# A streaming encoder step on one core: rope by copies, normalised tiles in step, and a first gate product in three passes

## What is computed

```
for i in range(2):
    x += 0.5 * swiglu(rmsnorm(x), w_ffn1)        # gate and up 1024 x 2816, down 2816 x 1024
    x += mixer_i(rmsnorm(x))                     # i = 0: latent attention, i = 1: retention
    x += 0.5 * swiglu(rmsnorm(x), w_ffn2)
y = rmsnorm(x)

def rope(x, pos):                                # x1, x2 are the halves of the last axis
    return concatenate([x1 * cos - x2 * sin, x1 * sin + x2 * cos])
```

## Time and profile before

| | |
|---|---|
| median of 3 runs | 1680.11 us (1679.96 to 1680.40) |
| the profiled execution, whole | 1680.21 us |
| its span, first to last instruction | 1678.4 us |
| PE busy | 1643.5 us, 98% of the span, 9523 matmuls |
| weight loads of PE | 1583.1 us, beside the matmuls |
| DVE busy | 822.8 us, 49% |
| ACT busy | 636.1 us, 38% |
| POOL busy | 287.4 us, 17% |
| mean granted clock of PE | 0.996 |
| share of PE in the chain that ended last | 94% |

### The profile page before, as it was taken

One profiled execution on the slowest core, in us unless ns is written; L12 is line 12 of the kernel. 1 busy time (PEld: TensorE's weight loads), 2 busy tenths in 40 slices (PEclk: granted clock), 3 DMA queues, 4 the chain that ended last, 5 costly groups with the idle time before them and its releaser, 6 DMA issues.

```text
span 1678.4 us, 25183 instructions
## 1 busy us (share of the span) xinstructions
PE 1643.5 (98%) x9523; PEld 1583.1 (94%) x9523; DVE 822.8 (49%) x969; ACT 636.1 (38%) x781; POOL 287.4 (17%) x263
## 2 busy tenths in 40 slices
PE   7999999999999999999999999999999999999997
PEld 6999999978899999999999999898989889999997
DVE  6444444654364444445444444574747476444332
ACT  5444322255334443224444323433333344444232
POOL 2111112440031111121111022202020222111021
PEclk9999999999999999999999999999999999999999
DMA  5444344451034444444444345656565654444342
GB/s 165 125 125 125 109 131 136 146 172 44 20 101 131 128 127 116 117 131 129 127 128 129 101 128 154 226 180 242 181 239 180 241 179 111 125 125 125 103 121 89
DMA packets 341737, 231.26 MB, mean 138 GB/s; under 512 B 8429, under 2 KB 312634, under 8 KB 341690
## 3 DMA queue, kind: packets, MB, share of 16 engines
q1 hardware_dynamic: 341690, 230.61, 45.7%
HBM read 209.64 MB, written 20.94 MB: 137 GB/s over the span
## 4 chain that ended last, share of the span: by engine, by line
PE 94%; DVE 3%; ACT 1%; DMA 1%; issue 1%; SPq 0%; POOL 0%; DVEq 0%; ACTq 0%; POOLq 0%
PE bank L140 27%; PE bank L142 27%; PE bank L141 27%; PE bank L1381 1%; PE bank L1382 1%; PE bank L1383 1%; PE bank L863 1%; PE bank L1418 1%; PE bank L1448 1%; DVE XL L152 1%; DMA RAW<-w_ffn_up_dram 1%; DVE WL L134 1%; PE bank L839 1%; PE bank L843 1%; PE bank L1489 1%
## 5 line engine op out<-in xcount | busy, mean ns | idle before, releaser
L140 PE MATMUL bank<-XH,WH 128*128 128x384 f32 x1776 | 599.9, 338 | 6.8 <-DVE XL L152 6.8
L142 PE MATMUL bank<-XH,WL 128*128 128x384 f32 x1776 | 595.1, 335 | 0.0
L141 PE MATMUL bank<-XL,WH 128*128 128x384 f32 x1776 | 595.0, 335 | 0.0
L127 ACT ACTIVATE WH<-RAW 128x2048 fp32r<-128x2048 f32 (+2 forms) x199 | 337.0, 1695 | 623.8 <-PE bank L142 579.3
L134 DVE TENSOR_TENSOR WL<-RAW,WH 128x2048 fp32r<-128x2048 f32 (+2 forms) x199 | 408.2, 2053 | 299.9 <-ACT WH L127 299.6
L140 PEld LDWEIGHTS bank<-XH,WH 128*128 128x128 f32 x1776 | 334.6, 188 | 14.4 <-issue 8.0
L141 PEld LDWEIGHTS bank<-XL,WH 128*128 128x128 f32 x1776 | 334.8, 188 | 1.1
L142 PEld LDWEIGHTS bank<-XH,WL 128*128 128x128 f32 x1776 | 334.6, 188 | 0.0
L140 PE MATMUL bank<-AH,WH 128*128 128x384 f32 x704 | 238.3, 339 | 0.0
L141 PE MATMUL bank<-AL,WH 128*128 128x384 f32 x704 | 237.8, 338 | 0.0
L142 PE MATMUL bank<-AH,WL 128*128 128x384 f32 x704 | 237.8, 338 | 0.0
(11 more groups left out here) (226 smaller groups left out, 1466.3 us busy)
## 6 DMA issues: line engine op xcount, KB each, us to landing
RAW<-w_ffn_gate_dram SPq DMA_DIRECT2D x88, 512.0 KB, 4.0
RAW<-w_ffn_up_dram SPq DMA_DIRECT2D x88, 512.0 KB, 5.2
RAW<-w_ffn_down_dram SPq DMA_DIRECT2D x64, 384.0 KB, 4.0
RAW<-w_ret_in_dram SPq DMA_DIRECT2D x48, 512.0 KB, 4.9
RAW<-w_ffn_down_dram SPq DMA_DIRECT2D x64, 320.0 KB, 3.3
st<-state_ret_dram SPq DMA_DIRECT2D x32, 512.0 KB, 7.0
new_state_sample_dram<-st SPq DMA_DIRECT2D x32, 512.0 KB, 6.3
RAW<-w_ret_out_dram SPq DMA_DIRECT2D x16, 512.0 KB, 4.4
```

Of the source, the lines that this page charges most:

```text
L127: ins = act.activation(dst(WH), src, ACT.Copy)
L140: pe.matmul(ps, wh, xh, start=first, stop=False)
L141: pe.matmul(ps, wh, xl, start=False, stop=False)
L142: return pe.matmul(ps, wl, xh, start=False, stop=last)
```

## The change

- **Rope.** `rotate` and its permutation are gone from PE. ACT copies the quarters of `pe_raw` crosswise into a new buffer `pe_swap` (4 copies of 32 partitions for a group, 2 for the key alone); the sign moves into the sine table; DVE multiplies `pe_swap` by it, in the list after part 0 of the next group. In `pe_prompt` the transposes take the banks in another order and wait only for the readings of their own bank.
- **Tiles in step with the output projections.** In Mla, XH and XL of the next block go to new buffers X2H and X2L, tile by tile behind the additions; the feed-forward block after it reads these. In the last head of Retention XL tiles follow the additions, and the split of the next block's first weights stands before the fourth XH tile on ACT.
- **Squares.** For these two norms ACT makes the squares (`square_act`), POOL only adds (`norm_adds_pool`).
- **First gate product pass by pass**, in all four feed-forward blocks: WH x XH for all k, WL x XH for all k, then WH x XL, waiting for XH in the first pass and for XL in the third. In the two blocks after a mixer PE first waits for the addition that frees the bank (`banks_free`).
- **SP at the end of Retention.** The next block's first load stands ahead of the first group of stores, the second load ahead of the second group.

The core of the diff:

```diff
+        def square_act(act, s, m):
+            if m >= 3:
+                act.wait_ge(sem("acc"), KD * s + m - 1)
+            act.activation(sq[:, m % 2, :] if m else acc[:, :], X[:, m, :], ACT.Square).then_inc(sem("sq" if m else "acc"), 1)
+        def norm_adds_pool(pool, s):
+            for m in range(1, KD):
+                pool.wait_ge(sem("sq"), (KD - 1) * s + m)
+                pool.wait_ge(sem("acc"), KD * s + m)
+                pool.tensor_tensor(acc[:, :], acc[:, :], sq[:, m % 2, :], ALU.add).then_inc(sem("acc"), 1)
...
-                            for k in range(KD):
-                                if first and j == 0 and part == 0:
-                                    pe.wait_ge(sem("xl"), KD * self.s + k + 1)
-                                mm = product(pe, ps[:, 0:T], w, k, XH[:, k, :], XL[:, k, :], k == 0, k == KD - 1)
+                            if first and j == 0 and part == 0:
+                                for k in range(KD):
+                                    pe.wait_ge(sem("xh"), KD * self.s + k + 1)
+                                    pe.matmul(ps[:, 0:T], w(WH, k), self.xh[:, k, :], start=(k == 0), stop=False)
+                                for k in range(KD):
+                                    pe.matmul(ps[:, 0:T], w(WL, k), self.xh[:, k, :], start=False, stop=False)
+                                for k in range(KD):
+                                    pe.wait_ge(sem("xl"), KD * self.s + k + 1)
+                                    mm = pe.matmul(ps[:, 0:T], w(WH, k), self.xl[:, k, :], start=False, stop=(k == KD - 1))
...
+                if self.banks_free:
+                    pe.wait_ge(sem(f"x_ready{self.s}"), self.banks_free)
                 gate_pair(0, True)
...
-                        if part == 1:
-                            rotate(g)
...
-                for i, ps in enumerate((gate_ps[0], gate_ps[1], up_ps[0], up_ps[1])):
+                for i, (ps, taken) in enumerate(((gate_ps[1], 15), (up_ps[1], 15), (gate_ps[0], 16), (up_ps[0], 17))):
+                    pe.wait_ge(sem("m_proj"), taken)
...
+                def swap(n):
+                    act.wait_ge(sem("m_proj"), 6 + 3 * n)
+                    if n >= 1:
+                        act.wait_ge(sem("m_turn_read"), n)
+                    for lo in range(0 if n else ROPE, P, ROPE):
+                        mid, hi = lo + ROPE // 2, lo + ROPE
+                        act.activation(pe_swap[lo:mid, :], pe_raw[mid:hi, :], ACT.Copy).then_inc(sem("m_swap"), 1)
+                        act.activation(pe_swap[mid:hi, :], pe_raw[lo:mid, :], ACT.Copy).then_inc(sem("m_swap"), 1)
...
+                swap(0)
                 for q in range(3, 7):
                     self.look_act(act, q)
+                    swap(q - 2)
...
-                for q in range(7, 6 + KD // 2):
-                    self.look_act(act, q)
                 act.wait_ge(sem("stored"), 16 * 2 * TT)
-                act.wait_ge(multiplied, self.c0 + self.N_CHUNKS)
-                for m in range(KD):
-                    norm_tile_act(act, self.s + 1, m, gain(KD * (self.s + 1) + m))
+                for g in range(KD // 2):
+                    norm_tile_act(act, self.s + 1, 2 * g, gain(KD * (self.s + 1) + 2 * g), xh=X2H)
+                    if g:
+                        square_act(act, self.s + 1, 2 * g - 1)
+                    if g < KD // 2 - 1:
+                        self.look_act(act, 7 + g)
+                    norm_tile_act(act, self.s + 1, 2 * g + 1, gain(KD * (self.s + 1) + 2 * g + 1), xh=X2H)
+                    square_act(act, self.s + 1, 2 * g)
+                square_act(act, self.s + 1, KD - 1)
...
+                    dve.wait_ge(sem("m_swap"), 2 + 4 * n)
+                    lo = 0 if n else ROPE
+                    dve.tensor_tensor(pe_sin[lo:P, :], pe_swap[lo:P, :], msin[lo:P, :], ALU.mult).then_inc(sem("m_turn_read"), 1)
...
+                        if m >= 2:
+                            norm_tile_dve(dve, self.s + 1, m - 2, gain(KD * (self.s + 1) + m - 2), X2H, X2L)
...
-                for group in range(3):
-                    store_states(RET_HEADS - 1, group)
+                self.next_ffn.load_gate(sp, 0, 0)
+                store_states(RET_HEADS - 1, 0)
+                self.next_ffn.load_gate(sp, 0, 1)
+                store_states(RET_HEADS - 1, 1)
+                store_states(RET_HEADS - 1, 2)
...
                 for m in range(KD):
+                    if m == 3:
+                        self.look_act(act, RET_HEADS - 1, 6)
                     norm_tile_act(act, self.s + 1, m, gain(KD * (self.s + 1) + m), self.x_base)
+                    if m:
+                        square_act(act, self.s + 1, m - 1)
...
                     if m == 3:
                         self.look_dve(dve, h, 6)
+                    if last and m >= 2:
+                        norm_tile_dve(dve, self.s + 1, m - 2, gain(KD * (self.s + 1) + m - 2))
```

More of the change, by code:

```diff
@@ L142, in product, with norm_tile_act, norm_tile_dve @@
             return pe.matmul(ps, wl, xh, start=False, stop=last)
[L146 removed]
+        def norm_tile_act(act, s, m, g, base=0, xh=XH):
             act.wait_ge(sem(f"x_ready{s}"), m + (base + 1))
[L148 to L150 removed]
+            act.activation(tile(xh, m), tile(X, m), ACT.Copy, scale=g).then_inc(sem("xh"), 1)
+        def norm_tile_dve(dve, s, m, g, xh=XH, xl=XL):
             dve.wait_ge(sem("xh"), m + (KD * s + 1))
[L152 removed]
+            dve.scalar_tensor_tensor(tile(xl, m), tile(X, m), g, tile(xh, m).bitcast(F32),
                                      ALU.mult, ALU.subtract).then_inc(sem("xl"), 1)
@@ L285, in sp @@
             def sp(self, sp):
-                first = 1 if self.c0 == 0 else 0
+                first = 1 if self.c0 == 0 or self.last else 0
                 with sp.Fori(first, KF // 2) as i:
@@ L627, in pe @@
                 projection(2, KD, XH, XL, two, False, q_sum)
-                def rotate(n):
-                    pe.wait_ge(sem("m_proj"), 6 + 3 * n)
-                    if n == 0:
-                        pe.wait_ge(sem("mtab_in"), 16)
-                    if n >= 1:
-                        pe.wait_ge(sem("m_turn_read"), n)
-                    pe.matmul(misc_ps[:, 0:T], rot, pe_raw[:, :], start=True, stop=True).then_inc(sem("m_turned"), 1)
                 for g in range(4):
@@ L1134, in dve @@
                            .then_inc(sem(f"x_ready{self.s + 1}"), 1)
-                    if g < KD // 2 - 1:
-                        self.look_dve(dve, 7 + g)
-                dve.wait_ge(sem("stored"), 16 * 2 * TT)
-                for m in range(KD):
-                    norm_tile_dve(dve, self.s + 1, m, gain(KD * (self.s + 1) + m))
+                        if part and g < KD // 2 - 1:
+                            self.look_dve(dve, 7 + g)
+                        if m == 2:
+                            dve.wait_ge(sem("stored"), 16 * 2 * TT)
+                        if m >= 2:
+                            norm_tile_dve(dve, self.s + 1, m - 2, gain(KD * (self.s + 1) + m - 2), X2H, X2L)
+                for m in (KD - 2, KD - 1):
+                    norm_tile_dve(dve, self.s + 1, m, gain(KD * (self.s + 1) + m), X2H, X2L)
                 self.look_dve(dve, 6 + KD // 2)
@@ L1521, in act, with act_head @@
                 norm_root_act(act, self.s + 1)
-            def act_head(self, act, h):
+            def act_head(self, act, h, last=False):
                 c = self.c0 + self.PER * h
@@ L1571, in act_head @@
                 z_hi(3)
-                for q in (5, 6):
-                    self.look_act(act, h, q)
+                self.look_act(act, h, 5)
+                if not last:
+                    self.look_act(act, h, 6)
             def dve(self, dve):
@@ L1585, in dve @@
                     self.look_dve(dve, h, self.PER - 1)
-                self.dve_head(dve, RET_HEADS - 1)
-                for m in range(KD):
+                self.dve_head(dve, RET_HEADS - 1, True)
+                for m in (KD - 2, KD - 1):
                     norm_tile_dve(dve, self.s + 1, m, gain(KD * (self.s + 1) + m))
@@ L1591, in dve, with dve_head @@
                 norm_root_dve(dve, self.s + 1)
-            def dve_head(self, dve, h):
+            def dve_head(self, dve, h, last=False):
                 c = self.c0 + self.PER * h
@@ L1769, in angles @@
         return np.cos(ang).astype(f), np.sin(ang).astype(f)
-    turn, half = np.zeros((P, P), f), ROPE // 2
-    for base in range(0, P, ROPE):
-        for i in range(half):
-            turn[base + half + i, base + i] = -1.0
-            turn[base + i, base + half + i] = 1.0
     cos, sin = angles(ROPE)
-    mla = np.concatenate([turn, np.tile(cos, (4, 1)), np.tile(sin, (4, 1))], axis=1)
+    mla = np.concatenate([np.tile(cos, (4, 1)), np.tile(np.concatenate([-sin, sin]), (2, 1))], axis=1)
     lg = np.log(f(1.0) - f(2.0) ** (-5.0 - np.arange(RET_HEADS, dtype=f))).astype(f).astype(np.float64)
```

53 lines of the change are left out of this document (26 added, 27 removed).

## The result

The changed kernel takes 1672.17 us (median of 5 runs, 1671.38 to 1673.48), the kernel before, on the same chip, 1680.18. The ratio is 0.9952, with a 95% interval of 0.9937 to 0.9966. It is faster, by 8.0 us where 13.3 were forecast, and 1672.2 lies above the range of 1664.8 to 1670.8. The profiled execution took 1672.17, with a span of 1670.4.

A forecast was written before the change was run, and what follows sets the result against it. PE (TensorE) was taken to set the end, so savings come off the span one for one: 3.0 + 8.0 + 2.7 - 0.4 = 13.3 us, from 1680.2 to 1666.9 us, range 1664.8 to 1670.8.

The forecast's parts named there:

- A: Handover from attention to feed-forward: tiles made beside the output products let the norm's sum start earlier, 3.0 us saved (2.5 to 3.1).
- B: Handover from retention to feed-forward: early first weight load and split remove PE's wait and half clock, 8.0 us saved.
- 0.3 for acc: Deduction at the retention handover: two POOL additions after the last square give acc at 1384.2 to 1384.5, against 1384.1 undisturbed.
- the 4.16 of the earlier trace: Handover scale between two feed-forward blocks with nothing to wait for: first gate product to norm's sum, 24 matmuls, 4.16 us.
- Rival 2: Retention handover: DVE is the bound with XL tiles at 1.12 us; gain 6.4 us, time 1668.5 us, chance 0.11.
- a margin of 0.4: After the retention handover: the weight split for the second pair would be ready about 0.4 us early; its loss under 1 us.
- C: Latent projections: five rotations leave PE, value products begin 3.6 us earlier, head loop earlier; 2.7 us saved (0.5 to 3.6).
- D: First gate product pass by pass: the last XH tile is asked for sooner, costing 0.4 us, 0.25 between feed-forward blocks.
- the 0.15 at the start: Pass-by-pass cost at the kernel's start, where the last XH tile is as tight as between feed-forward blocks: 0.15 us.
- Rival 1: Latent projections give nothing: POOL held by a further split, or PE at half clock; 1669.6 or 1670.6 us, chance 0.13.
- the 4.06 that stood ahead of the half clock: PE's idle time of 4.06 us before the half clock at the old retention handover, used as the scale for gaps.
- the 1.3 of my chain: Latent projections, around the transposes: no single PE gap was predicted over 1.3 us, so the clock was expected to hold.

## Why the prediction was off

**What bounds the kernel** was right: PE sets the end, and all four parts act by what they do to its list. The error was in what a matmul costs. I took 0.173 us from the earlier trace rows and wrote "matmul count and weight loads stay", and from this that the block behind the attention costs the same. The count stayed, and the price didn't: 176.0 ns instead of 173.3. It is half of the 5.3 us by which the forecast missed. The step that failed belongs to handover A: moving the tiles to the new tensors X2H and X2L was put at nothing, without a reason, and it costs 2.75 us. Without it the time would have been 1669.4, inside the range. The trace of before had the hint, since matmuls on AH, of the same shape, came 176.0 ns apart and those on XH 173.5; I read only those on XH.

**A** itself was right: 2.8 measured, 3.0 forecast. The sum began 4.7 us after the last output product, where I had put 4.2 to 4.7. What is missing is XH 7, which I had just in time and which costs 0.33. By an estimate from the rows, product by product PE would have asked for XL 7 at about 485.9, and it was done at 484.39; so behind the attention the passes seem to cost this 0.33 and gain nothing. No run tests them there alone. (I also counted A's handover from the end of the last product, 0.34 after its start, and B's from the next start, 0.17 after it, so A was 0.17 short on B's measure.)

**B** gave 6.9 for 8.0. The mechanism was right, each step of the early load is in the timeline, the clock is 1.00 in each stage, and no store stands among PE's waits. Mis-sized was the one term taken off, 0.3 for acc: the handover takes 1.38 more than the 4.16 of the earlier trace rows. XH 7 makes 0.70 of this, which I had at 0.1, and the sum 0.54. I had counted two additions behind the last square; POOL was already behind by then, for the squares come every 1.0 us and an addition takes 1.28. The additions on POOL cost 0.99 of the 1.38: beside them an XL tile takes 1.16 instead of my 0.71 to 0.88, and one of 0.90 on DVE holds up the last addition to X and with it XH 7. Rival 2, which had tiles of 1.12 and 6.4 us, is nearer in number, 0.5 off against 1.1, but by luck: in its chain PE is held by the XL tiles, and PE waited for none of them. The pair for the second gate product, where I left a margin of 0.4, had no wait.

**C** gave 1.5 for 2.7. The value products came 2.8 earlier counted from the query sum instead of 3.6, and 1.3 instead of 0.9 went again behind them. The last rope addition, which I had at 354.4, ended at 355.11, or 355.7 on the scale of the kernel before, counted from the query sum. I let a pair of additions cost 1.7 beyond the split that it waits for. By itself it takes 2.05; two pairs stood beside a split (4.03 and 3.99), DVE's sine products waited for them (0.43 and 0.88), and where the pair had started first the split was stretched too: 2.72 and 2.65 instead of 2.29. Where the split had started first, it took 2.28. The rule that I had cited, of the Trainium skill, "SBUF — State Buffer" (section "SBUF: two separate sides"), gives the pair of ports to whoever starts first, and this agrees; what was missing is that I charged POOL for it and not VectorE. The copies on ACT, which I had bounded by 0.51, took 0.52.

**D** cost 0.36 between the feed-forward blocks, forecast 0.25 (766.05 less 765.85 in its own rows is 0.20), and 0.38 came back when it was undone there. Of the 0.15 at the start nothing can be said, for the first sum differs more than that between kernels with the same code there.

**Rival 1** had the clock right in kind. It didn't fall in the changed kernel (1.00 in all stages of the attention, where the longest gap of the stage is 1.11). My reason against it leaned on the 4.06 that stood ahead of the half clock, and that was weak: in the run with the additions on VectorE it fell after gaps of 1.87, 0.98 and 1.91, each less than half of that. Two of them are still longer than the 1.3 of my chain, so whether gaps up to that length could do it stays open. The Trainium skill's "TensorE: Matmul & The Clock Gate" (section "What's actually happening") has the gate go by how busy PE was recently; that run is in keeping with it and doesn't prove it.

Together: 2.75 for X2, 1.2 for C, 1.1 for B and 0.2 for A make 5.2 of the 5.3; the rest is what the small terms and the two ends leave. The range missed as well, for it was built from waits alone and held nothing for a change in the pace of the work that stays. Its other errors, 2.5 us together, would have stayed within it.

## What to carry to other kernels

When a change gives a matmul another operand, compare in the trace of before the spacing of equal matmuls on different tensors, not only their count: here 1.5% of a matmul's time hung on where a tensor starts. Place what PE reads as moving operand so that it starts equally far past a multiple of 256 bytes as the weights; one pad of 128 bytes a partition brought 6.8 us here, a second pad and one condition 2.1 more, together more than the whole change. Then look at the spacing on every tensor that the pad has moved, since one of them may have been in a good place. And where VectorE and GpSimd both read two SBUF tensors, charge both engines for each overlap, and look for who queues behind the longer one.

## What the chip showed that I had not expected

- The spacing of matmuls with 384 columns is 173.3 ns when the moving operand and the weights start equally far past a multiple of 256 bytes, and 175.6 to 176.0 ns when they differ by 128. Other differences give no simple order: 96 in both halves (zh, zl) was the slowest, 176.6, while 224 in both (173.5) and the pair 16 and 128 (173.3) were as fast as equal places. Why is open: that the weight load beside the matmul reads the same memory is a guess that fits the run with the weights moved, but no run shows it. The Trainium skill, "SBUF — State Buffer" (section "Who interferes with whom"), calls TensorE's two read ports independent and says that it never waits on anyone. Here the two readers of TensorE itself don't look independent, and the measurement decides.
- Beside retention weights the mean spacings on XH and XL, by pair of operands, lie between 173.3 and 177.1 ns from 1070 to 1375 us, in both kernels and in those with moved tensors; that was not followed up.
- A pair of additions of 64 x 384 on GpSimd takes 2.05 us alone and 3.99 beside a split on VectorE, which itself goes from 2.28 to 2.65 when the pair has started first and stays at 2.28 when the split has.
